# Gate halves over both attentions, an output granule between the channel means, and the third norm's token factor behind the products

## Chip, cores, metric

One NeuronCore of a Trainium2 chip runs the whole program. Its engines are TensorE (PE, with its weight loads as PEld), VectorE (DVE), ScalarE (ACT), GpSimd (POOL) and SyncE (SP, which only starts transfers). The metric is the device time of one execution in microseconds.

## What is computed

Two transformer blocks on 256 tokens of width 1024, everything in float32, cut here to what the change touches:

```python
# first block
h = rmsnorm(x, norm_mix)                       # first norm
y_a = dilated_mixture(qa, ka, va)              # attention "A", 8 heads
y_b = indexed_sparse_attention(qb, kb, vb, qi, ki, wi)   # attention "B", 64 best keys of each query
merged = sigmoid(h @ w_ga) * (y_a @ w_up_a) + sigmoid(h @ w_gb) * (y_b @ w_up_b)
x = x + merged @ w_out
h = rmsnorm(x, norm_ffn)                       # second norm
x = x + (silu(h @ w_gate) * (h @ w_up)) @ w_down
x = rmsnorm(x, norm_final)
# second block
h = rmsnorm(x, norm1_g)                        # third norm
q, k, v, a, gate = split(h @ w_in)             # q and k are normed by head and rotated
attn = attention(q, k, v)                      # attention "G", 8 query heads, 2 key heads
c = silu(layernorm(conv31(a * sigmoid(gate)))) # 512 channels, 31 taps
x = x + concat([attn, c]) @ w_out
hn = rmsnorm(x, norm2_g)
x = x + experts(hn)       # 8 heads choose 16 of 16384 rows of u and of v each
x = rmsnorm(x, final_g)
```

## The kernel before

**Precision.** A float32 product is made of three products of parts: each weight granule (128 x 2048, 1 MB, in the order of the list `GRANULES`) is loaded by SP into one of three `raw` buffers, ACT copies it to `w_hi` (`prepare`), POOL subtracts to get `w_lo` (`low_part` of POOL, four pieces), and PE multiplies high by high, high by low and low by high. The activations are split likewise, by ACT or DVE (`high_of_...`) and DVE (`low_of_...`). Only the query weights of the experts are used whole.

**Order.** Each engine runs its own program in order; semaphores tie them together. PSUM has eight banks. `plan_psum` writes down the order in which PE fills which bank, and `ps.start`, `ps.full`, `ps.empty` and `ps.copied` wait and signal by that plan; the orders of the engines are written out by hand. DVE and ACT queue whatever stands behind a wait.

**Attentions.** `attention(kind, ...)` exists on PE, DVE and ACT and goes through eight units (two tiles of 128 tokens, four pairs of heads). In step s PE makes the scores, transposes the probabilities of unit s - 1, and multiplies them by the values at steps 3, 5, 8 and 9; the factors of the softmax are turned at steps 6 and 9. DVE takes the maxima, ACT the exponentials. In A, DVE also picks the best keys for B (`select_round`). Beside this PE computes the gates (`gate_half`, two halves of 24 products to a granule) and the first part of the up products (`up_products`, 12 products each); `gate_beside` says which half goes with which step: in A one in every step 0 to 8, in B in steps 0 to 6, then `up_products` in steps 7 and 8 and behind. In G, PE also does 28 of the taps of the fourth group of channels, DVE most of the others, POOL 16 taps of the third group; `mean_of_conv` and `var_of_conv` form the layer norm's sums on PE, and DVE subtracts the mean and multiplies.

**Third norm.** `both_sums` on ACT forms the sums of squares of x and of x times `norm_final` (called `hn`); the product of the final norm of the first block and of the third norm is one factor for each token. DVE scales `hn` by it (`down_norm`, `scaled_tokens`), PE turns the scaled tokens (`turn_piece(2, ...)`, with small products of `keep_warm` in the meantime), DVE multiplies by the gain of each channel, and the parts feed the products `kv2`, `conv0` to `conv3` and `q2`. DVE's `conv_input` writes a times the sigmoid; `head_roots` (ACT) and `head_norm` (DVE) norm the heads.

**Behind G.** `out2` is the output product of the second block, granules `wp0` to `wp3`, each by tile of tokens (`high_tokens`, `out_products`). Then come the queries and the experts: DVE chooses, POOL gathers 128 rows of 4 KB with each instruction, DVE forms the dot products with u, PE adds the rows of v.

## Time and profile before

| | us |
|---|---|
| median of three runs | 1261.77 (1257.54 to 1262.18) |
| the profiled execution, its time | 1261.23 |
| the profiled execution, its span | 1259.3 |

| engine | busy us | share of the span |
|---|---|---|
| PE | 1036.7 | 82% |
| PEld | 673.7 | 53% |
| DVE | 772.0 | 61% |
| ACT | 412.1 | 33% |
| POOL | 885.1 | 70% |

The profile is one execution. Engines work side by side, so the shares don't add up. A line of a timeline gives the start in us from the span's beginning, the length, the engine, the line of the kernel, the operation with output and inputs, how many instructions were merged (x8), and in brackets the idle time of the engine before it with what ended it. Ends of matmuls are modelled. The granted clock is the share of TensorE's full 2.4 GHz that was granted (0.50 is 1.2 GHz throughout). Rough stages: first projections to 82 us, A to 120, B to 157, up and output products to 205, feed-forward to 390, third norm and second projections to 437, G to 474, output and queries to 595, experts to the end; the first gather starts at 493.58.

### The profile page before, as it was taken

The numbers are of one execution on the slowest core, as the hardware profiler recorded it, in microseconds if no ns is written. First come the engines' busy times: TensorE is split into PE (matmuls) and PEld (weight loads), VectorE is DVE, ScalarE is ACT, GpSimd is POOL, SyncE is SP. The second block draws the span as 40 slices with busy tenths as digits, with TensorE's granted clock in tenths as the row PEclk, the third lists the DMA queues.
The fourth block names the chain that finished last, engine by engine and source line by source line (L and its number), as shares of the span: only waits on it lengthen the run. The fifth ranks groups of instructions, "written<-read, shape, count | busy, mean of one in ns | idle before, by whom it ended". The sixth has DMA issues, their size and how long they took to land.

```text
span 1259.3 us, 13029 instructions
## 1 busy us (share of the span) xinstructions
PE 1036.7 (82%) x4236; PEld 673.7 (53%) x4236; DVE 772.0 (61%) x1708; ACT 412.1 (33%) x764; POOL 885.1 (70%) x827
## 2 busy tenths in 40 slices
PE   7999899999999989768887868568595785856875
PEld 7889788888888967757332323223141331322322
DVE  4466344566797786558875845547484663655445
ACT  5466655443437563113031121202121021221231
POOL 6866487999996893554757667676676766757664
PEclk9999999999999999878988879688796987979889
DMA  7634255554554427887999999899999989989997
GB/s 272 200 135 147 89 168 188 181 199 172 196 205 164 163 105 263 292 329 262 352 339 406 341 348 399 331 410 332 381 369 347 401 336 360 391 333 409 345 360 312
DMA packets 89727, 356.80 MB, mean 283 GB/s; under 512 B 9680, under 2 KB 9808, under 8 KB 82384
## 3 DMA queue, kind: packets, MB, share of 16 engines
q0 software_dynamic: 73728, 268.47, 55.6%
q1 hardware_dynamic: 15520, 86.15, 19.5%
q10 hardware_dynamic: 432, 1.57, 0.3%
q8 instruction: 27, 0.44, 0.1%
q14 instruction: 20, 0.16, 0.0%
HBM read 355.10 MB, written 1.05 MB: 283 GB/s over the span
## 4 chain that ended last, share of the span: by engine, by line
PE 34%; POOL 25%; issue 21%; DVE 8%; another core or an unknown queue 6%; DMA 4%; ACT 1%; POOLq 0%; SPq 0%; DVEq 0%; ACTq 0%
PE bank L1359 9%; POOL u_row L2727 9%; POOL v_row L2727 8%; POOL w_lo L2678 8%; PE bank L903 7%; PE bank L905 3%; DVE u_row L2510 3%; PE bank L738 3%; PE bank L739 3%; PE bank L740 3%; PE bank L825 2%; DMA u_row<-peer_u_dram,expert 1%; DMA v_row<-peer_v_dram,expert_of_v 1%; PE bank L1278 1%
## 5 line engine op out<-in xcount | busy, mean ns | idle before, releaser
L1359 PE MATMUL bank<-v_row,diag 128*128 128x512 f32 x928 | 463.5, 645 | 168.1 <-issue 147.3
L1359 PEld LDWEIGHTS bank<-v_row,diag 128*128 128x128 f32 x928 | 187.7, 205 | 443.5 <-issue 418.7
L2678 POOL TENSOR_TENSOR w_lo<-raw,w_hi 128x512 fp32r<-128x512 f32 (+1 forms) x280 | 367.2, 1352 | 80.1 <-ACT w_hi L1498 80.0
L2510 DVE CUSTOM_DVE_ANT_0 u_row<-u_row,bank 128x1024 f32<-128x1024 f32 x256 | 301.7, 1213 | 89.5 <-DMA u_row<-peer_u_dram,expert 55.4
L2727 POOL DMA_INDIRECT v_row<-peer_v_dram,expert_of_v x240 | 231.2, 963 | 157.2 <-remote 81.0
L2727 POOL DMA_INDIRECT u_row<-peer_u_dram,expert x256 | 244.6, 956 | 116.0 <-issue 73.4
L1793 ACT ACTIVATE diag<-consts,mixw 128x128 f32<-128x128 f32 x256 | 79.4, 389 | 504.5 <-remote 352.3
L1498 ACT ACTIVATE w_hi<-raw 128x2048 fp32r<-128x2048 f32 x71 | 135.8, 1912 | 74.0 <-PE bank L740 29.1
L903 PE MATMUL bank<-hT_high_and_low,w_hi 128*128 128x512 f32 x352 | 124.6, 399 | 0.0
L905 PE MATMUL bank<-hT_high_and_low,w_lo 128*128 128x256 f32 x352 | 98.8, 281 | 0.0
L903 PEld LDWEIGHTS bank<-hT_high_and_low,w_hi 128*128 128x128 f32 x352 | 66.1, 188 | 16.6 <-POOL w_lo L2678 0.6
L905 PEld LDWEIGHTS bank<-hT_high_and_low,w_lo 128*128 128x128 f32 x352 | 66.5, 189 | 0.0
L738 PE MATMUL bank<-hT_high_and_low,w_hi 128*128 128x256 f32 x192 | 55.8, 290 | 0.0
L740 PE MATMUL bank<-hT_high_and_low,w_lo 128*128 128x256 f32 x192 | 54.3, 283 | 0.0
L739 PE MATMUL bank<-hT_high_and_low,w_hi 128*128 128x256 f32 x192 | 54.3, 283 | 0.0
L825 PE MATMUL bank<-w_hi,hT_high_and_low 128*128 128x512 f32 (+1 forms) x224 | 50.2, 376 | 0.0
L1288 PE MATMUL bank<-hT_whole,raw_late 128*128 128x256 f32 x160 | 39.6, 397 | 11.0 <-issue 11.0
L825 PEld LDWEIGHTS bank<-w_hi,hT_high_and_low 128*128 128x128 f32 x224 | 39.5, 188 | 8.0 <-issue 0.7
L1288 PEld LDWEIGHTS bank<-hT_whole,raw_late 128*128 128x128 f32 x160 | 31.5, 199 | 17.6 <-issue 13.8
L2201 DVE TENSOR_REDUCE ff_up<-bank 128x256 f32<-128x512 f32 x22 | 15.2, 690 | 38.9 <-PE bank L905 38.9
L738 PEld LDWEIGHTS bank<-hT_high_and_low,w_hi 128*128 128x128 f32 x192 | 36.6, 190 | 2.0 <-issue 1.5
L739 PEld LDWEIGHTS bank<-hT_high_and_low,w_hi 128*128 128x128 f32 x192 | 36.6, 191 | 0.0
(300 smaller groups left out, 1468.5 us busy)
## 6 DMA issues: line engine op xcount, KB each, us to landing
raw<-stream_dram SPq DMA_DIRECT2D x74, 1024.0 KB, 4.8
u_row<-peer_u_dram,expert POOLq DMA_INDIRECT x256
v_row<-peer_v_dram,expert_of_v POOLq DMA_INDIRECT x240
raw_late<-stream_dram SPq DMA_DIRECT2D x3, 1024.0 KB, 4.9
raw_late<-stream_dram SPq DMA_DIRECT2D x4, 512.0 KB, 6.1
residual<-x_in_dram SPq DMA_DIRECT2D x2, 512.0 KB, 4.0
out_dram<-residual SPq DMA_DIRECT2D x4, 256.0 KB, 2.2
consts<-consts_in_dram SPq DMA_DIRECT2D x1, 840.0 KB, 10.6
```

Of the source, the lines that this page charges most:

```text
L738: mm(out_ap, left[0], right[0], start=first, stop=False, skip_group_check=resumed)
L739: mm(out_ap, left[0], right[1], start=False, stop=False, skip_group_check=resumed)
L740: return mm(out_ap, left[1], right[0], start=False, stop=last, skip_group_check=resumed)
L825: mm(out, x[:, k, t * P:(t + 1) * P], w, start=first and k == chunks[0] and x is source[0], stop=False)
L903: mm(bank[:, :].rearrange("p (s t) -> p s t", s=2), high, hT_both[:, :, k, :], start=k == 0, stop=False, skip_group_check=True)
L905: ins = mm(bank[:, 0:T], low, hT_hi[:, k, :], start=False, stop=k == KD - 1, skip_group_check=True)
L1359: ins = mm(accs[half][:, :], diag[:, 2 * m + i, :], row[:, half * 512:(half + 1) * 512], start=False, stop=True, skip_group_check=True)
L1498: activation(w_hi[parts_slot(n)][:, :], raw[n % RING][:, :], ACT.Copy).then_inc(high_done, 1)
L1793: ins = activation(diag[:, i, :], ident, ACT.Copy, scale=mixw[:, i:i + 1])
L2510: ins = v.tensor_tensor_reduce(out=row_of_u, in0=row_of_u, in1=hn_tile[:, :], scale=1.0, scalar=0.0, op0=ALU.mult, op1=ALU.add, accum_out= ...
L2678: ins = nc.gpsimd.tensor_tensor(w_lo[r][:, cols], source[:, cols], w_hi[r][:, cols].bitcast(F32), ALU.subtract)
L2727: nc.gpsimd.indirect_dma_start(rows[2 * m + i][:, :], None, table_in, bass.IndirectOffsetOnAxis(ap=named[:, b, 2 * m + i:2 * m + i + 1], a ...
```

## The change

It has three parts. (1) Of the 16 gate halves, A takes seven (steps 0 to 4, 6 and 8) instead of nine, B nine instead of seven; `up_products(0, 0)` moves to B's step 9, the next two behind the loop, and ACT's `prepare("up1")` from step 7 to the end of step 8. (2) PE turns the unscaled `hn`, its first two turns among the last products of `w_down`; `high_of_norm(2)` on ACT moves ahead of the sums of the last piece, `prepare("conv1")` behind all sums. The token factors are formed later: DVE writes two diagonal blocks, one product spreads them to all rows (`factor_rows`), DVE copies them to `factors`; `conv_scale` multiplies both halves of each conv bank by them, v and the heads' norm take the factor as a scalar, ACT's squares as `scale`. (3) `out2` of tile 0 starts its first granule (high parts of the tokens, both parts of `wp0`) between the two halves of the channel means in G's step 7; `high_of_y("G", 0, 0)` goes ahead of that step's exponentials. Nothing is left out of the computation.

```diff
@@ -223,15 +223,12 @@
...
 PAIRED = "ABG"
-GATE_FROM = {"A": 0, "B": 9}
-UP_BESIDE = {7: 0, 8: 1, 9: 2}
+GATE_STEPS = [("A", s) for s in (0, 1, 2, 3, 4, 6, 8)] + [("B", s) for s in range(9)]
...
-    if kind == "G" or s > 8 or GATE_FROM[kind] + s >= NGATE:
-        return None
-    return divmod(GATE_FROM[kind] + s, 2)
+    return divmod(GATE_STEPS.index((kind, s)), 2) if (kind, s) in GATE_STEPS else None
...
@@ -296,8 +293,8 @@
...
                 ps.plan("D", ("gate", gate_beside(kind, s)[0]))
-            if kind == "B" and s in (7, 8):
-                ps.plan("D", ("up", UP_BESIDE[s]))
+            if (kind, s) == ("B", 9):
+                ps.plan("D", ("up", 0))
             if (kind, s) == ("A", 0):
...
@@ -782,11 +782,13 @@
...
                     ps.copied(pe, ("out", t, half))
+                elif i == 2:
+                    pe.wait_ge(gained, 2 * t + half + 1)
                 else:
-                    pe.wait_ge(normed, TT * i + 2 * t + half + 1)
+                    pe.wait_ge(normed, 2 * t + half + 1)
                 name = ("norm", i, t, half)
                 bank = ps.start(pe, name)
-                tokens_in = X if i == 1 else xs
+                tokens_in = (xs, X, hn)[i]
                 for c in range(4):
...
@@ -980,8 +982,8 @@
...
                         scores_ahead()
-                    if kind == "B" and s in (7, 8):
-                        up_products(UP_BESIDE[s], 0)
+                    if (kind, s) == ("B", 9):
+                        up_products(0, 0)
                     if kind == "G" and s == 8:
...
@@ -1002,8 +1004,12 @@
...
                         mean_of_conv(0)
+                        ps.start(pe, ("out2", 0, 0))
+                        pe.wait_ge(y_high, 2 * 2 + 1)
+                        high_tokens(0, 0)
                 if kind == "B":
-                    up_products(2, 0)
+                    for c in (1, 2):
+                        up_products(c, 0)
...
@@ -1164,6 +1190,7 @@
...
             for half in range(2):
+                turn_piece(2, 0, half)
                 done = down_part(last - 1, 1, half)
...
@@ -1187,9 +1214,6 @@
...
-            for half in range(2):
-                turn_piece(2, 0, half)
-            keep_warm(BRIDGE[2][1])
             low_part("kv")
...
@@ -1203,8 +1227,11 @@
...
             ps.fill(kv_low(1, 1), ("kv2", 1))
+            pe.wait_ge(factors_known, 2)
+            mm(y_bank[:, 0:T], mean_w, xs[:, 1, 0:T], start=True, stop=True).then_inc(factor_rows, 1)
             for c in range(2):
                 pair(f"conv{c}", ("conv", c))
+            pe.wait_ge(factors_copied, 1)
             tokens("q2", ("q20", "q21"), hT)
...
@@ -1308,10 +1315,10 @@
...
             ps.copied(pe, ("y", "G", 0))
-            for q in range(2):
-                ps.start(pe, ("out2", 0, q))
-                high_tokens(q, 0)
-                out_products(q, 0, "low tokens")
+            out_products(0, 0, "low tokens")
+            ps.start(pe, ("out2", 0, 1))
+            high_tokens(1, 0)
+            out_products(1, 0, "low tokens")
             pe.wait_ge(conv_high, 1)
...
@@ -1465,6 +1472,8 @@
...
                         prepare("conv0", 0)
+                    if (t, half) == (1, 1):
+                        high_of_norm(2)
                     ps.copied(act, ("down", t, half))
...
@@ -1503,8 +1512,6 @@
...
                         continue
-                    if i == 2 and (t, half) == (1, 0):
-                        prepare("conv1", 0)
                     act.wait_ge(ht_full, 4 * i + piece + 1)
...
@@ -1528,6 +1535,8 @@
...
                 for s in range(len(todo) + 1):
+                    if (kind, s) == ("G", 7):
+                        high_of_y(kind, base, 0)
                     if s < len(todo):
...
@@ -1542,7 +1551,7 @@
...
                         high_of_y("A", 0, 1)
-                    if s == 7:
+                    if s == 7 and kind != "G":
                         high_of_y(kind, base, 0)
...
@@ -1567,7 +1576,7 @@
...
                         prepare(f"wp{s}", 0)
-                    if kind == "B" and s == 7:
+                    if kind == "B" and s == 8:
                         prepare("up1", 0)
...
@@ -1671,13 +1680,14 @@
...
             both_sums()
-            high_of_norm(2)
+            prepare("conv1", 0)
...
                     prepare(f"conv{c}", ahead)
-                bank = ps.full(act, ("conv", c))
+                bank = ps.bank(("conv", c))
+                act.wait_ge(conv_scaled, c + 1)
                 activation(conv_b[:, c, :], bank[:, T:2 * T], ACT.Sigmoid).then_inc(conv_sig, 1)
...
@@ -1687,9 +1697,10 @@
...
                     act.wait_ge(head_sum_done, n - 1)
-                activation(relu[:, n % 2, 0:cols], bank[:, 0:cols], ACT.Square).then_inc(head_sq_done, 1)
                 if n == 0:
                     act.wait_ge(final_rstd, 1)
+                activation(relu[:, n % 2, 0:cols], bank[:, 0:cols], ACT.Square, scale=column(rstd, TT * 3 + t)).then_inc(head_sq_done, 1)
+                if n == 0:
                     activation(X[:, 0, :], hn[:, 0, :], ACT.Copy, scale=column(rstd, TT * 2)).then_inc(x_scaled, 1)
...
@@ -2249,27 +2260,25 @@
...
-            def down_norm(t):
-                norm_scale(TT * 3 + t, TT * 2 + 2 * t + 1)
-                scaled_tokens(t, hn, TT * 3 + t)
             down_tile(0)
-            down_norm(0)
-            down_tile(1)
             for half in range(2):
...
                               ps.bank(("norm", 2, 0, half))[:, :].rearrange("p (c t) -> p c t", c=4)).then_inc(ht_high, 1)
-            down_norm(1)
-            low_of_norm(2, 0, 0)
-            gain_of_norm(2, 0, 1)
-            low_of_norm(2, 1, 0)
-            gain_of_norm(2, 1, 1)
+            for half in range(2):
+                low_of_norm(2, half, 0)
+            down_tile(1)
+            for half in range(2):
+                gain_of_norm(2, half, 1)
             for half in range(2):
                 low_of_norm(2, half, 1)
+            for t in range(TT):
+                norm_scale(TT * 3 + t, TT * 2 + 2 * t + 1)
+            for t in range(TT):
+                ins = v.tensor_scalar(xs[:, 1, t * P:(t + 1) * P], ident, column(rstd, TT * 3 + t), float(CC * P), ALU.mult, ALU.mult)
+            ins.then_inc(factors_known, 1)
             dve.wait_ge(root_done, TT * 4)
...
@@ -2281,6 +2290,7 @@
...
                 settle(v.reciprocal(head_rstd[:, b, 0:heads], head_root[:, b, 0:heads]))
+                settle(v.tensor_scalar(head_rstd[:, b, 0:heads], head_rstd[:, b, 0:heads], column(rstd, TT * 3 + n % TT), None, ALU.mult))
                 whole = bank[:, 0:heads * HD].rearrange("p (h w) -> p h w", w=HD)
...
@@ -2304,9 +2314,15 @@
...
             settle(v.memset(conv_in[:, :, PAD + T:], 0.0))
+            def conv_scale(c):
+                bank = ps.full(dve, ("conv", c))
+                both = bank[:, :].rearrange("p (s t) -> p s t", s=2)
+                v.tensor_tensor(both, both, row(factors, 2, T), ALU.mult).then_inc(conv_scaled, 1)
...
-                bank = ps.full(dve, ("conv", c))
+                bank = ps.bank(("conv", c))
                 dve.wait_ge(conv_sig, c + 1)
...
@@ -2315,7 +2331,7 @@
...
                 dve.wait_ge(head_sq_done, t + 1)
-                v.tensor_copy(v2[:, t, :], bank[:, 2 * HD:4 * HD])
+                v.tensor_scalar(v2[:, t, :], bank[:, 2 * HD:4 * HD], column(rstd, TT * 3 + t), None, ALU.mult)
                 head_norm(t, bank, 2)
...
@@ -2324,6 +2340,11 @@
...
                 rotated_from(("kv2", t))
+            dve.wait_ge(factor_rows, 2)
+            settle(v.tensor_copy(factors[:, :], y_bank[:, 0:T]))
+            v.memset(flag[:, :], 0.0).then_inc(factors_copied, 1)
+            for c in range(2):
+                conv_scale(c)
             conv_input(0)
...
@@ -2335,8 +2356,10 @@
...
             for c in range(2, CC):
+                conv_scale(c)
+                conv_taps(2)
                 conv_input(c)
-                conv_taps(4)
+                conv_taps(2)
             attention("G", 2, None)
...
```

The hunks left out are the plan of the PSUM banks (`out2` of tile 0 moves from banks 0 and 2 to 2 and 0, the names behind it accordingly), two semaphores, and `out_products` and `high_tokens`, which move unchanged to where step 7 of G can call them.

## Rows read from the trace of the kernel before

**Rows 1.** Windows view, two stretches: length, busy us (instructions), granted clock, DMA share, GB/s
```profile
163.00:384.00 221.00, 220.35 (x1206) 190.07 (x1205) 145.97 (x179) 99.49 (x93) 202.64 (x151) 1.00 0.53 187
...
493.50:1259.30 765.80, 561.05 (x1364) 262.06 (x1362) 459.69 (x1152) 151.19 (x383) 491.99 (x512) 0.85 0.92 352
```

**Rows 2.** Timeline: start, length, engine, line, operation, out, in; POOL's first gather
```profile
493.58 1.15 POOL L2727 DMA_INDIRECT u_row<-peer_u_dram,expert  x1 [17.33 <-PE bank L1233]
```

**Rows 3.** Timeline of PE, ACT and DVE in the first attention, steps 5 and 6
```profile
101.10 0.36 PE L738 MATMUL bank<-hT_high_and_low,w_hi 128*128 128x256 f32 x1
...
104.06 0.60 PE L913 MATMUL bank<-consts,E_sb 128*128 128x128 f32 x4
...
102.39 0.36 ACT L1565 ACTIVATE PT<-bank 128x256 f32<-128x256 f32 x1
...
106.39 0.69 DVE L2076 SCALAR_TENSOR_TENSOR S_sb<-bank,consts 128x512 f32<-128x512 f32 x1 [1.14 <-issue]
...
109.24 0.41 DVE L2017 MATCH_REPLACE8 score<-little,score 128x256 f32<-128x256 f32 x1
```

**Rows 4.** Timeline of ACT, POOL and PE at the end of the second attention
```profile
152.12 1.90 ACT L1498 ACTIVATE w_hi<-raw 128x2048 fp32r<-128x2048 f32 x1
...
154.40 0.60 ACT L1592 ACTIVATE full<-bank 128x512 f32<-128x512 f32 x1
...
154.10 9.91 POOL L2678 TENSOR_TENSOR w_lo<-raw,w_hi 128x512 fp32r<-128x512 f32 x8 [15.13 <-ACT w_hi L1498]
...
153.53 0.66 PE L913 MATMUL bank<-consts,rden_wide 128*128 128x128 f32 x4
...
159.10 0.39 PE L738 MATMUL bank<-yT_hi,w_hi 128*128 128x256 f32 x1 [3.36 <-POOL w_lo L2678]
```

**Rows 5.** Waits of PE, 119 to 164 us: us in total, times, longest
```profile
PE bank L913 <- ACT E_sb L1539: 0.7, 1, 0.7
...
PE bank L1040 <- DVE yT_lo L2142: 0.5, 1, 0.5
```

**Rows 6.** Windows view of the five microseconds after PE's wait
```profile
160.00:165.00 5.00, 5.00 (x33) 5.00 (x33) 1.18 (x3) 2.30 (x2) 4.01 (x4) 0.72 0.68 210
```

**Rows 7.** Timeline of the third norm: roots on ACT, kv products on PE
```profile
394.18 0.48 ACT L1434 ACTIVATE root<-sumsq,var 128x1 f32<-128x1 f32 x2
...
394.28 0.71 PE L1181 MATMUL bank<-w_hi,hT_high_and_low 128*128 128x256 f32 x4 [0.26 <-DVE hT_high_and_low L2264]
...
401.47 0.64 PE L1187 MATMUL bank<-w_hi,hT_high_and_low 128*128 128x256 f32 x4
```

**Rows 8.** Timeline of DVE and POOL between the convolution's products
```profile
398.36 0.68 DVE L1910 TENSOR_TENSOR bank<-bank,params 128x512 f32<-128x512 f32 x1
...
415.07 7.53 DVE L656 SCALAR_TENSOR_TENSOR bank<-conv_in,params,bank 128x256 f32<-128x256 f32 x19
...
437.44 0.43 DVE L2311 TENSOR_TENSOR conv_in<-bank,conv_b 128x256 f32<-128x256 f32 x1 [4.06 <-ACT conv_b L1681]
...
432.17 0.94 POOL L2710 TENSOR_SCALAR conv_p<-conv_in,params 128x256 f32<-128x256 f32 x1
```

**Rows 9.** Timeline of PE, DVE, ACT and POOL at the third attention's end; one window
```profile
466.33 1.79 PE L1062 MATMUL bank<-conv_a,consts 128*128 128x256 f32 x4 [1.66 <-DVE conv_a L2124]
...
468.00:470.00 2.00, 2.00 (x11) 1.29 (x11) 1.81 (x4) 1.93 (x3) 2.00 (x3) 0.50 0.87 369
...
464.42 1.43 DVE L2122 TENSOR_TENSOR conv_a<-conv_a,conv_p 128x256 f32<-128x256 f32 x1
...
468.88 1.23 ACT L1602 ACTIVATE conv_b<-conv_a 128x512 f32<-128x512 f32 x2
...
476.83 0.64 ACT L1735 ACTIVATE yT_hi<-conv_b 128x512 fp32r<-128x512 f32 x1
...
460.62 15.63 POOL L2678 TENSOR_TENSOR w_lo<-raw,w_hi 128x512 fp32r<-128x512 f32 x12
...
479.47 1.07 PE L1233 MATMUL bank<-w_hi,yT_hi 128*128 128x512 f32 x4
```

## What I predict, and from what

> **What bounds the kernel now.** I read the table of stretches first, then for each stretch that the change touches what ended PE's idle time, then the timelines of all engines there. From 163 to 384 us PE is busy 220.35 of 221 us, from 493.5 to the end the 16 DMA engines are busy 0.92 of the time at 352 GB/s [rows 1]. So the span has two regimes. Up to the first gather PE sets the pace, with short stretches in which VectorE (DVE) or a chain through ScalarE (ACT) and GpSimd (POOL) does; every microsecond at 163 us arrives at 384, since PE stands for 0.65 us in between. After the first gather, at 493.58 [rows 2], the memory traffic is the clock, and its volume is untouched: I let a shift of the first gather pass one for one. The sum is therefore the shift of three places: PE's product of `up2` at 159.10, the start of the third attention at about 439.5, and the first gather. All numbers are of the profiled execution: span 1259.3, time 1261.23; the median of the three runs is 0.54 more, and I add the shift to that median, 1261.77.
>
> **Part 1, gate halves.** The two halves at steps 5 and 7 of the first attention leave it; the second gets them, in its steps 7 and 8, and `up0` and `up1` move behind. PE's work is the same. A half is 24 products, from 101.10 to the transpose at 104.06, 3.0 us [rows 3]; two are 6.0. What covers their place? At step 5 PE would reach the values of units 0 and 1 at 101.8, but ACT copies the fourth unit's probabilities until 102.75 [rows 3]: 1.0 idle. At step 7 the transpose waits for a bank's copy, 0.5. DVE takes 3.26 us a unit for the scores and two rounds of selection (106.39 to 109.65) [rows 3], and moves up only 1.1 us, since it was already busy; its next unit starts at about 110.0 and frees the bank that the second scores of B need at 110.7: 1.1 idle. Bank and copy waits at the end add 0.4. So of 6.0 us 3.0 come back as idle time, and PE enters the second attention 3.0 us earlier. The bounds are 0 and 6.0 us.
>
> In the second attention the added halves only cover what is idle there, but `up1` is split later. Before, ACT wrote its high part at 152.12, ahead of the copy of the last factor (154.40), POOL began at 154.10 and PE got it at 159.10 after 3.36 us of waiting [rows 4]. Now the high part stands behind the copy of that factor, and this copy waits for PE's transpose of the factor, which comes behind two gate halves and `up0`. It began at 153.53 [rows 4]; now 3.0 us earlier from A, 6.0 later for the two halves, 1.5 earlier because `up1` (12 products) goes behind it, and 1.2 earlier because the waits of 0.7 and 0.5 us [rows 5] are covered: 153.8, ending at 154.4. Queued behind the waiting copy on ACT are the high parts of `up1` and `up2`; for the first POOL waits, and PE for POOL. Copy 0.6, high part 1.98 to POOL's start, split 4.96 (half of the 9.91 us of eight pieces) [rows 4]: 162.0. PE has values and `up1`'s first half, 2.5 us, to put beside 7.6, and then waits 5.1 us. That is 2.9 us later than 159.10. With no gain in A it would be 5.9, with all of it -0.1. The granted clock, at its full 2.4 GHz before, was on average 0.72 in the 5 us after this wait [rows 6], so the products ran partly at 1.2 GHz; the longer wait brings the same fall, and it cancels. **Part 1: +2.9 us**, passed on to 384.
>
> **Part 2, the third norm.** Removed: the wait of the transposes for root, reciprocal and scaling, and the small products that keep PE busy meanwhile; the scalings themselves give way to two small ones. Two transposes of 0.45 us go between the last products of `w_down`, which end 1.0 us later. From there: kv of tile 0 at 391.3 instead of 394.28 [rows 7], transposes of tile 1 at 393.2, and the last kv product ends at 397.9 instead of 401.95 [rows 7]: 4.0 us gained. Then the change adds a wait: the factors come from the roots, which ended at 394.66 [rows 7] and now, with two copies of 0.6 us and a wait for the transposes ahead of the second half's squares, at 398.3; with a reciprocal and two scalings of 0.24 us 398.9. PE stands 1.0 us, behind it the whole of `conv0`, which then starts at 399.2, 2.7 early. `conv1` is split by 405.3 and its high part no longer precedes the roots; with 48 products of 0.12 us each and 0.3 us of waiting for that split, it ends at 411.0.
>
> DVE then takes this away. The two new `conv_scale(0)`, `conv_scale(1)` stand ahead of `conv_input(0)`, so DVE waits for `conv1` (411.05), with the first 8 taps queued behind, which had run beside `conv1`'s products. A scaling of 128x512 in PSUM has no row; the nearest is the gain multiply, 0.68 us [rows 8], bounded by the 0.43 of half the size below and by the 1.43 of the slow DVE add above [rows 8, 9]; I take 0.7. From 411.05: 0.7, input 0.4, 8 taps 4.2, input 0.4, 20 taps 8.0 (7.53 us for 19) [rows 8] = 424.9 against 422.6. Two query tiles at 4.35 + 0.2 for the added small product give 434.0, two scalings, two inputs and 8 taps 5.7: 439.8, against 439.5 (the input at 437.44 and four taps). The 4.06 us that DVE had waited for `conv3` [rows 8] are eaten up; PE, with `conv3` done at 434.5, waits for the turned queries. The rest of the additions (factor on v, ACT's `scale`, one product of 0.28 us) lies on the same instructions or beside others. ACT's copy of the keys now stands behind the sigmoid of `conv2` and ends at 435.7, still ahead. **Part 2: +0.3 us**, bounds -4.0 (the PE gain passes) and +3.8.
>
> The side effect is POOL's. It starts its 16 taps when `conv_input(2)` has freed the bank: 436.0 instead of 432.17 [rows 8], so it ends them at 464.5 instead of 460.62, and DVE's add of its part began at 464.42 [rows 9]. The wait costs 0.1 at most; behind it POOL splits `wp1` to `wp3`, done at 480.1 instead of 476.25 [rows 9]. There is no slack left at the join.
>
> **Part 3, the granule.** Eight products (1.8 us) go between the two means, where PE waited 1.66 us for DVE [rows 9]. y's high part is ready at 463.5 (it precedes the exponentials now, 0.5 us of ACT that no one misses), the granule ends at 466.9, 0.4 after the second mean could start. The granted clock was 0.50 in 468 to 470, and the second mean's four products took 1.79 us [rows 9]; with the gap filled I take them at 1.1. The variances wait for ACT's squares, from 468.88 on [rows 9], at the earliest 469.5 and 470.1: the second ends at 471.2 instead of 472.4. The rest follows: values, low tokens, `wp1` until 476.3, conv's high part at 476.4 instead of 477.4 (ACT), so `wp2` starts at 476.45 instead of 479.47 [rows 9]; 3.0 early. `wp3`'s low part is there at 480.1, needed at 480.1. With the 0.4 and the nearness of POOL I take **-2.5 us**, bounds -3.3 and +0.4.
>
> DVE's add of two SBUF operands of 128x256 took 1.43 us beside POOL, a multiply of that size with one operand in PSUM 0.43 [rows 8, 9]. The Trainium skill ("SBUF — State Buffer", section "SBUF: two separate sides") calls the shared port pair of DVE and GpSimd an exclusive lock: the loser waits for the whole instruction. It speaks against this change, because the later splits now lie beside `low_of_conv(0)`, which is on the path. By the row's excess, 1.0 us, part 3 would be -1.5; without it -2.5.
>
> **Sum:** +2.9 + 0.3 - 2.5 = +0.7 us: 1262.5.
>
> **Rivals.**
> - The norm's gain passes: if DVE's 4.06 us of waiting and POOL's chain hold more than I count, part 2 is -4.0: 1261.77 + 2.9 - 4.0 - 2.5 = 1258.2. For it: DVE is the only thing between; against it: the taps are counted instruction by instruction.
> - Everything passes: selection does not hold PE in A and `up1` meets PE, part 1 -0.1: 1255.2. Against it: the copy of the factor stands ahead of `up1` in ACT's program.
> - The join (ends slower): POOL meets DVE at 464.5 without slack. If four of DVE's instructions between 411 and 436 lose 0.95 us each (about the excess of the slow row [rows 9]), the second conv input comes 3.8 later, past the join, POOL's `wp3` at 484 swallows part 3: 2.9 + 0.3 + 3.8 = +7.0, 1268.8. It decides from the moment `conv_input(2)` ends after 435.9. Against it: these instructions have a PSUM operand.
> - The change does not do what it says: in A the halves had covered selection entirely, PE gains nothing, part 1 is +5.9: 1265.5; or the clock falls all the same at 466 and part 3 gives 0.
>
> **Chances.** Forecast 0.46 (its own range 1259 to 1266), norm's gain passes 0.14, everything passes 0.12, the join 0.10, the last 0.18. Faster by over 0.5% (6.3 us, about what a measurement here can tell from no change) means under 1255.5: everything passes, and a little of its neighbour, 0.14. Slower means over 1268.1: 0.11. Within: 0.75. The three runs spread over 4.6 us. The range reaches from the everything case to the join case: 1255 to 1268.5.
>
> **What would show it.** Part 1: PE's first `up2` product at about 162, the wait for POOL near 5 us, and 1 us waits on copies and scores in A. Part 2: kv done by 398 + 2.9, DVE without idle time between 411 and 440 (+2.9), first maximum of G near 442.6. Part 3: no 0.50 clock at the second mean, `wp2` three us closer to it. The first gather near 494.3. Wrong would be: `up2` before 160, DVE waiting for `conv3`, POOL's taps past DVE's join, or an expert stage that is not 766 us long.

## The result and the profile after

| | us |
|---|---|
| median before, same chip | 1260.36 (1257.54 to 1265.61) |
| median after | 1265.09 (1258.98 to 1271.49) |
| ratio after to before | 1.0034, 95% interval 1.0018 to 1.0050 |
| the profiled execution after, its span | 1260.9 |

The changed kernel is 4.3 us slower (0.0034 of 1260.36; the two medians alone differ by 4.7), less than the 0.5% that the forecast called no change. I had forecast +0.7 us, and the difference lies almost wholly in one of the three parts.

The profiled span grew by 1.6 us only (1259.3 to 1260.9), since the two executions differ where the change does nothing. The windows view of after, the two stretches of [rows 1] (length, busy us, granted clock, DMA share, GB/s):

```profile
163.00:384.00 221.00, 218.62 (x1198) 189.03 (x1199) 141.65 (x176) 99.04 (x90) 206.05 (x154) 0.99 0.54 187
499.30:1260.90 761.60, 569.91 (x1364) 265.73 (x1362) 459.98 (x1151) 150.27 (x383) 491.44 (x512) 0.83 0.92 354
```

The stage of the experts took 761.6 us instead of 765.8, at 354 GB/s instead of 352; and the first attention began at 86.63 us in after and 85.37 in before, though nothing had changed up to there. So I read every kernel by its first gather, less the start of its first attention. In before that is 493.58 - 85.37 = 408.21 us, in after 499.31 - 86.63 = 412.68: **4.47 us later**, which agrees with the medians. All shifts below are formed so ("net"), from one profiled execution each, against before.

```profile
499.31 1.16 POOL L2750 DMA_INDIRECT u_row<-peer_u_dram,expert  x1 [10.85 <-PE bank L1063]
```

**Part 1 in after.** The timeline of PE in the first attention (start, length, engine, line, operation, count, idle time before and what ended it), and in a second fence the windows behind the waits:

```profile
110.20 0.63 PE L915 MATMUL bank<-consts,E_sb 128*128 128x128 f32 x4 [0.39 <-ACT PT L1574]
110.76 0.71 PE L969 MATMUL bank<-kT,qT_qb 64*128 64x128 f32 x4
111.98 0.71 PE L969 MATMUL bank<-kT,qT_qb 64*128 64x128 f32 x4 [0.52 <-DVE S_sb L2087]
```

```profile
112.00:115.00 3.00, 3.00 (x17) 2.88 (x18) 2.83 (x9) 2.31 (x7) 0.00 (x0) 0.68 0.32 134
...
164.50:168.00 3.50, 3.44 (x17) 3.44 (x18) 0.00 (x0) 2.29 (x2) 3.50 (x4) 0.54 0.67 179
```

The waits are the forecast ones (1.1 us ahead of 104.15, then 0.39 and 0.52). New is the granted clock of 0.68 behind them: the gate half from 112.62 to 117.26 took 4.6 us instead of 3.1, and 1.5 of the 3.0 us gained were gone. At the second up granule PE waited 4.87 us for POOL (forecast 5.1).

**Part 2 in after.** DVE's query tiles, POOL beside them, and PE at the start of the third attention:

```profile
432.24 0.44 DVE L2293 TENSOR_SCALAR head_rstd<-head_rstd,rstd 128x8 f32<-128x8 f32 x1
...
437.06 1.19 DVE L2293 TENSOR_SCALAR head_rstd<-head_rstd,rstd 128x8 f32<-128x8 f32 x1
...
434.42 5.03 POOL L2701 TENSOR_TENSOR w_lo<-raw,w_hi 128x512 fp32r<-128x512 f32 x4 [1.77 <-ACT w_hi L1507]
...
443.02 0.63 PE L915 MATMUL bank<-consts,rotated 128*128 128x128 f32 x4 [0.94 <-ACT kT L1726]
443.58 1.13 PE L969 MATMUL bank<-kT,qT_qi 64*128 64x256 f32 x4
445.76 1.13 PE L969 MATMUL bank<-kT,qT_qi 64*128 64x256 f32 x4 [1.05 <-DVE conv_in L2327]
446.81 4.97 PE L1107 MATMUL bank<-conv_in,tap_diag 128*128 128x256 f32 x14
...
454.62 0.69 DVE L2081 TENSOR_REDUCE negmax<-bank 128x2 f32<-128x512 f32 x1 [2.05 <-PE bank L969]
```

Two things weren't in the forecast. A multiplication of 128x8 numbers took 0.44 and 1.19 us. And PE stood twice for about 1 us, its 14 taps then took 4.97 us (3.29 in the kernel before), and DVE waited 2.05 us for the next scores.

**Part 3 in after.** PE between the means:

```profile
472.49 1.13 PE L1088 MATMUL bank<-conv_a,consts 128*128 128x256 f32 x4 [1.61 <-DVE little L2125]
473.27 1.27 PE L1063 MATMUL bank<-w_hi,yT_hi 128*128 128x512 f32 x4
474.38 1.08 PE L1063 MATMUL bank<-w_lo,yT_hi 128*128 128x512 f32 x4
475.30 1.02 PE L1088 MATMUL bank<-conv_a,consts 128*128 128x256 f32 x4
...
485.10 1.15 PE L1063 MATMUL bank<-w_hi,yT_hi 128*128 128x512 f32 x4
```

The granule fills the gap, the second mean takes 1.02 instead of 1.79 us [rows 9], and `wp2` starts 11.72 us after DVE's addition of the conv parts (485.10 - 473.38; before 479.47 - 464.42 = 15.05): 3.3 us gained.

### The profile page after: what moved, and what is told of

Read it like the earlier page. It is cut to its first block, busy times and chain, and to the rows that moved or that the text cites. A ratio compares the mean times of both kernels' runs of the same rounds, so it can differ in the third digit from the quotient of the medians.

```text
span 1260.9 us, 12991 instructions
## 1 busy us (share of the span) xinstructions
PE 1046.8 (83%) x4214; PEld 676.9 (54%) x4214; DVE 775.2 (61%) x1716; ACT 411.4 (33%) x764; POOL 886.1 (70%) x827
## 3 DMA queue, kind: packets, MB, share of 16 engines
HBM read 355.10 MB, written 1.05 MB: 282 GB/s over the span
## 4 chain that ended last, share of the span: by engine, by line
PE 24%; issue 23%; DVE 23%; POOL 17%; another core or an unknown queue 8%; DMA 2%; ACT 1%; DVEq 0%; POOLq 0%; SPq 0%; ACTq 0%
DVE u_row L2533 11%; POOL w_lo L2701 11%; PE bank L905 6%; PE bank L1366 5%; POOL u_row L2750 4%; PE bank L907 3%; POOL v_row L2750 3%; PE bank L738 2%; PE bank L739 2%; PE bank L740 2%; DVE bank L656 1%; PE bank L1107 1%; DMA v_row<-peer_v_dram,expert_of_v 1%; PE bank L1285 1%
```

## The experiments

Shifts in us, net, against before. "Up" is PE's first wait behind the up products (166.92 in before), "G" the first maximum of the third attention (439.48), "join" DVE's addition of the conv parts (464.42), "gather" the first gather (493.58). The ratio is that of the times measured. 1' is part 1 with the early split of e4; "order", "filling" and "fold" are the edits of e6, e5 and e9, told below.

| kernel | parts | up | G | join | gather | ratio (95%) |
|---|---|---|---|---|---|---|
| after | 1, 2, 3 | +4.1 | +5.8 | +7.7 | +4.5 | 1.0034 (1.0018 to 1.0050) |
| e1_gate_only | 1 | +2.9 | +3.0 | +3.0 | +3.1 | 1.0020 (1.0003 to 1.0037) |
| e2_norm_only | 2 | 0.0 | +1.6 | +5.1 | +4.3 | 1.0032 (1.0009 to 1.0056) |
| e3_granule_only | 3 | 0.0 | +0.3 | +0.3 | -2.7 | 0.9996 (0.9977 to 1.0014) |
| e4_up_split_early | 1', 2, 3 | -3.5 | -1.8 | +1.7 | -1.7 | 0.9984 (0.9961 to 1.0008) |
| e5_norm_warm | 2, filling | 0.0 | +1.6 | +4.0 | +3.0 | 1.0015 (1.0006 to 1.0024) |
| e6_norm_order | 2, order | +0.7 | +1.8 | +5.3 | +4.3 | 1.0019 (1.0009 to 1.0030) |
| e7_gate_granule_early_split | 1', 3 | -3.6 | -3.4 | -3.4 | -5.2 | 0.9938 (0.9925 to 0.9952) |
| e8_all_mended | 1', 2, 3, order, filling | -3.5 | -2.6 | -0.2 | -1.5 | 0.9974 (0.9961 to 0.9986) |
| e9_norm_fold | 2, fold | +0.7 | +0.6 | +0.9 | -0.2 | 0.9994 (0.9962 to 1.0027) |
| e10_norm_fold_order | 2, fold, order | +0.8 | -1.0 | -0.8 | -1.6 | 0.9975 (0.9946 to 1.0004) |
| e11_all_mended_fold | 1', 2, 3, fold, order, filling at the mean | -3.6 | -4.9 | -4.7 | -6.7 | 0.9945 (0.9919 to 0.9971) |
| e12_no_norm_warm_mean | 1', 3, filling at the mean | -3.6 | -3.3 | -3.3 | -3.7 | 0.9960 (0.9930 to 0.9991) |

e5 to e8 ran on another chip, on which the experts' stage moved 403 GB/s and the kernel before took 1170.16 us; up to the first gather the timelines there have the same durations. e1 to e4 and e9 to e12 ran on two others (1264.48 and 1264.40 us before). The small shifts at "up" where part 1 isn't in (+0.7, +0.8) are the length of the slow clock behind the same wait of 3.36 us; a shift of 0.8 us is therefore the noise of this table. At the gather the three parts alone sum to 3.1 + 4.3 - 2.7 = +4.7, and the whole change gave +4.5. On the way they agree less well: at "up" after is 1.2 us later than e1, and between G and the join it loses 1.9 us where e2 loses 3.6. The clock fell in other places and for other lengths, and part of the agreement at the end is luck.

### Each part alone

e1, e2 and e3 are the kernel before with one part of the diff above each, nothing else.

> The kernel before with part 1 alone: the gate halves of steps 5 and 7 of the first attention moved to steps 7 and 8 of the second, the products of up0 and up1 behind them. Everything is taken net of the start of the first attention. My theory after reading the changed kernel's trace: the first product of the second up granule comes 4.2 us later than in the kernel before, 2.9 of it the sum of the prediction (waits of about 1.1, 0.4 and 0.5 us in the first attention, a wait of about 4.9 us for GpSimd at the end of the second), 1.3 to 1.5 because the granted clock falls behind those small waits, so that the gate half after them takes about 4.6 us instead of 3.1. The kernel ends 4 us later, ratio about 1.003. Rival, the prediction's own sum: 2.9 us, the gate half takes 3.1 and the clock stays at 1.00 between 112 and 117 us.

Measured: +2.7 us at PE's first product of the second up granule (162.64 - 86.23 against 159.10 - 85.37), +2.9 behind the up products, +3.1 at the gather. The rival, the prediction's own sum, was right; my theory, that the clock falls here too, was wrong. A window of e1 in the first attention, and PE's line at the end of the second:

```profile
112.00:115.00 3.00, 3.00 (x26) 2.88 (x25) 2.79 (x10) 2.71 (x7) 0.00 (x0) 1.00 0.18 74
```

```profile
162.64 0.58 PE L736 MATMUL bank<-yT_hi,w_hi 128*128 128x256 f32 x1 [4.88 <-POOL w_lo L2677]
```

Behind the same three small waits (0.51 us the longest here, 0.52 in after) the clock stayed at 1.00. So the 0.68 in after is not a property of the change: behind the same idle time the clock fell in one execution and not in another. The other five kernels with part 1 (e4, e7, e8, e11, e12) had it at 1.00 too.

> The kernel before with part 2 alone: the third norm's token factor applied behind the products. My theory: PE gains 3 to 4 us at the last product of kv, and VectorE's chain takes it away: the first maximum of the third attention comes 1.4 us later than before, and the first gather some 3 us later, because the granted clock falls again while the first taps of the third attention run (after two waits of about 1 us at its start). Rival, the prediction's sum: +0.3 us and no fall of the clock. A second rival: the clock fall in the changed kernel needs part 1's shift of the transfers; then +1.4 at the first gather.

Measured: +1.6 at G, +5.1 at the join, +4.3 at the gather (some 3 expected); the theory held, and the fall of the clock needs nothing of part 1. PE and DVE of e2 at the start of the third attention, and two windows there:

```profile
438.22 0.63 PE L917 MATMUL bank<-consts,rotated 128*128 128x128 f32 x4 [0.94 <-ACT kT L1722]
438.78 1.13 PE L971 MATMUL bank<-kT,qT_qi 64*128 64x256 f32 x4
440.95 2.00 PE L971 MATMUL bank<-kT,qT_qi 64*128 64x256 f32 x4 [1.04 <-DVE conv_in L2323]
442.89 5.74 PE L1085 MATMUL bank<-conv_in,tap_diag 128*128 128x256 f32 x14
448.46 0.60 PE L917 MATMUL bank<-consts,E_sb 128*128 128x128 f32 x4
...
451.46 0.69 DVE L2077 TENSOR_REDUCE negmax<-bank 128x2 f32<-128x512 f32 x1 [3.69 <-PE bank L971]
```

```profile
442.00:444.00 2.00, 2.00 (x6) 1.17 (x5) 2.00 (x6) 1.22 (x5) 1.79 (x3) 0.50 0.91 279
444.00:446.00 2.00, 2.00 (x6) 1.59 (x5) 2.00 (x6) 0.56 (x3) 1.76 (x3) 0.50 1.06 430
```

Two waits of about 1 us, then six microseconds at 1.2 GHz, in which the scores take 2.00 instead of 1.13 us and the taps 5.74 instead of 3.29. DVE, which bounds this stage, stands for 3.69 us.

From the join to the gather e2 wins 0.9 us back, although part 2 changes nothing there. POOL and DVE of e2 at the join show why:

```profile
469.22 1.27 POOL L2697 TENSOR_TENSOR w_lo<-raw,w_hi 128x512 fp32r<-128x512 f32 x1
...
470.21 0.56 DVE L2129 TENSOR_TENSOR conv_a<-conv_a,conv_p 128x256 f32<-128x256 f32 x1
```

The addition that I count as the join took 1.43 us in before [rows 9] and 0.56 here. In all 14 traces it took between 0.56 and 1.51 us and ended 0.27 to 0.29 us after the end of the splitting instruction that POOL was running. So up to 0.9 us of a shift at the gather depend on how far POOL has got with that instruction when DVE arrives.

> The kernel before with part 3 alone: the first output granule's products on the high part between the two channel means. My theory: from VectorE's add of the conv parts to the first product of wp2 3.3 us are gained, so that the first gather is 3.0 to 3.3 us earlier than before, net of the start of the first attention. Rivals: the prediction's -2.5, -1.5 if the shared port lock of the page on SBUF takes 1 us on low_of_conv, and 0 if the clock falls between the means all the same.

Measured: 0.3 at the join, -2.7 at the gather, so 3.0 us gained, the lower end of the theory and 0.5 more than the prediction. DVE's `low_of_conv(0)`, for which one rival priced POOL at 1 us, took 1.01 us instead of 0.69 in before: 0.3 us, and none in e7, which has part 3 as well (0.69).

### The late split

e4 is the changed kernel with

```diff
-                    if kind == "B" and s == 8:
+                    if kind == "B" and s == 7:
                         prepare("up1", 0)
```

> The changed kernel with one number different: ScalarE writes the high part of the second up granule at the end of step 7 of the second attention, as before the change, instead of behind the copy of the last factor in step 8. My theory: the high part is there some 4 us earlier, GpSimd's split ends before PE arrives, the wait of 4.9 us goes and with it the clock of 0.54 behind it: the first up2 product 4.5 to 5 us earlier than in the changed kernel and a first gather 5 us earlier, so the kernel is slightly faster than the one before. Rival: the split then delays the copy of the last factor and with it y, so that 2 us or more of waiting stay (gain 2 to 3 us). Second rival: the time saved comes back as idle time of PE before 384 us (gain 0).

Measured: the wait of 4.9 us is gone; PE goes through all up products from 157.57 to 165.02 without a break, at a clock of 1.00 from 160 to 164.5, and its next wait is this one:

```profile
165.70 0.36 PE L738 MATMUL bank<-yT_hi,w_hi 128*128 128x256 f32 x1 [0.69 <-DVE merged_lo L2175]
```

That is 7.6 us earlier than in after at "up" (+4.1 to -3.5): 4.9 for the wait, and the rest the slow clock behind it and in A. At the gather 6.1 us arrive, 5 had been expected; whether the kernel is faster than before, its interval (0.9961 to 1.0008) leaves open. What the forecast took for the price of moving two gate halves was the price of one number in ACT's program.

### The clock at the start of the third attention

e5 is e2 with small products whose result nobody reads:

```diff
+            warm_in(("scores",) + units("G")[0], 6)
             ps.copied(pe, ("turn", "k2"))
             turn_queries("q2", 1, 13, tiles=(1,))
             for u in range(2):
                 scores("G", 2, qT["q2"], keys_of_g, u)
+                if u == 0:
+                    warm_in(("probs",) + units("G")[0], 7)
```

> The kernel before with part 2 alone, as in e2_norm_only, and with 13 small products whose result nobody reads in PE's two waits at the start of the third attention (0.94 us for the copy of the turned keys, 1.04 us for the last conv_input). Times net of the start of the first attention, against the kernel before. In e2_norm_only the granted clock was 0.50 from 442 to 448 us, VectorE then waited 3.69 us for the scores of the third unit, and the join of the conv parts was 5.12 us late. My theory: the idle time of those two waits brings the clock down; with it filled the clock stays at 1.00, the wait of 3.69 shrinks under 0.5 us, the join is 1.6 us late and the first gather 0.8 us. Rival: the clock follows something else (the transfers of 400 GB/s that run at that time), the fall stays and the join is 5.1 us late again. Second rival: the taps wait for conv_input all the same, and VectorE's 3.69 us are part of that: join 3.5 to 4 us late at a clock of 1.00.

PE of e5 (L781 is the filling):

```profile
438.95 1.60 PE L781 MATMUL bank<-consts 128*128 128x128 f32 x12 [1.03 <-DVE conv_in L2331]
440.39 0.60 PE L917 MATMUL bank<-consts,rotated 128*128 128x128 f32 x4
440.92 1.13 PE L971 MATMUL bank<-kT,qT_qi 64*128 64x256 f32 x4
441.98 1.83 PE L781 MATMUL bank<-consts 128*128 128x128 f32 x14
443.74 1.13 PE L971 MATMUL bank<-kT,qT_qi 64*128 64x256 f32 x4
444.79 3.29 PE L1085 MATMUL bank<-conv_in,tap_diag 128*128 128x256 f32 x14
```

The clock was 1.00 in every stretch from 436 to 450 us, beside transfers of 400 GB/s, so the transfers are not what brings it down. But the join is 4.0 late, not 1.6. The second rival had that number, by another cause: I had mis-sized the filling. The first group began only when the wait was over (its bank came free at the same moment) and added 1.60 us, the second took 1.83 instead of 1.04. From the second scores to the next transpose PE needed 4.2 us (443.74 to 447.92) instead of 7.5 in e2 (440.95 to 448.46): the slow clock had cost 3.3 us, and the filling, which put the second scores 2.2 us later, took that much of it away again.

The nine kernels with part 2 agree on the clock. In the four in which PE stood for both waits (after, e2, e4, e6: 0.93 to 1.84 us and 1.04 to 1.05) it fell to 0.50 behind them; in the two with the filling, and in e9 to e11 below, whose only wait there is 0.40 to 0.57 us, it stayed at 1.00.

### The order of DVE's chain

```diff
-            for c in range(2):
-                conv_scale(c)
+            conv_scale(0)
             conv_input(0)
-            conv_taps(lead)
+            conv_taps(lead - 2)
+            conv_scale(1)
+            conv_taps(2)
             conv_input(1)
```

> The kernel before with part 2 alone, and in it VectorE's conv_input(0) and six taps ahead of conv_scale(1), instead of both scalings ahead of conv_input(0). My theory: the wait of 2.10 us for the products of conv1 in VectorE goes, since the taps of conv0 cover it, and conv_input(1) comes 1.5 to 2 us earlier than in e2_norm_only, net of the start of the first attention; PE's wait of 1.21 us ahead of q2 goes; the first maximum of the third attention is 0 to 0.5 us later than before the change instead of 1.57. PE's waits there remain, so the clock falls and the join is still 3 to 4 us late. Rival: the sigmoid's wait for the scaling, now in the open, eats the gain and nothing changes. Second rival: with VectorE earlier PE does not wait for conv_input, the clock stays up, and the join is 0 us late or earlier than before.

Half a hit. DVE's wait of 2.10 us went, and PE's of 1.21 ahead of `q2`; `conv_input(1)` came 1.1 us earlier than in e2 (1.8 less the shift of 0.7 at "up"). Yet G was as late as in e2, which only the first rival had said, for another reason. The gain vanished in the multiplication by the token factor in the head norm, which took 2.29 and 0.62 us in the two query tiles (0.44 and 1.19 in e2). POOL and DVE of e6:

```profile
424.90 6.32 POOL L2698 TENSOR_TENSOR w_lo<-raw,w_hi 128x512 fp32r<-128x512 f32 x5
...
426.46 2.29 DVE L2289 TENSOR_SCALAR head_rstd<-head_rstd,rstd 128x8 f32<-128x8 f32 x1
```

POOL's five instructions follow each other every 1.25 us and end at 426.2, 427.5, 428.7, 430.0 and 431.2. DVE's small one ends at 428.75, with one of them. The same in e2, POOL and DVE, twice:

```profile
401.44 8.82 POOL L2697 TENSOR_TENSOR w_lo<-raw,w_hi 128x512 fp32r<-128x512 f32 x7 [3.77 <-ACT w_hi L1505]
...
425.30 2.55 POOL L2697 TENSOR_TENSOR w_lo<-raw,w_hi 128x512 fp32r<-128x512 f32 x2
...
399.68 0.48 DVE L2276 TENSOR_SCALAR normed_tokens<-consts,rstd 128x128 f32<-128x128 f32 x2
...
403.08 0.95 DVE L2289 TENSOR_SCALAR head_rstd<-head_rstd,rstd 128x2 f32<-128x2 f32 x1
...
427.44 0.44 DVE L2289 TENSOR_SCALAR head_rstd<-head_rstd,rstd 128x8 f32<-128x8 f32 x1
```

POOL's pair ends at 427.85, DVE's instruction at 427.88. At 399.68 POOL is idle (3.77 us before 401.44), and the same operation on 128x128, 16 times the size of 128x8, takes 0.24 us. In the six kernels that have them (after, e2, e4, e5, e6, e8) all 24 of these small instructions end 0.02 to 0.04 us behind the end of one of POOL's. I read it so: such a `tensor_scalar` with both operands in SBUF waits until POOL is through with its running instruction (in e6 and e8 once with a second one, for which I have no reason); beside it the reciprocals of the same column took 0.17 to 0.20 and those with an operand in PSUM their usual 0.7 us. The Trainium skill ("SBUF — State Buffer", section "SBUF: two separate sides", under "Who interferes with whom") says that `tensor_scalar` between two places in SBUF can enter a mode that takes the port pair shared with GpSimd, as an exclusive lock held for a whole instruction. These rows agree with it. I had cited this lock in the prediction, but only for `low_of_conv(0)` in part 3, where it cost 0.3 us at the most. At the small instructions of part 2 I had not looked for it.

### The fold

e9 is e2 with that factor multiplied in along with the heads' own, in PSUM; e10 has the order of e6 as well.

```diff
-                settle(v.tensor_scalar(head_rstd[:, b, 0:heads], head_rstd[:, b, 0:heads], column(rstd, TT * 3 + n % TT), None, ALU.mult))
                 whole = bank[:, 0:heads * HD].rearrange("p (h w) -> p h w", w=HD)
-                settle(v.tensor_tensor(whole, whole, each(head_rstd[:, b, 0:heads], heads, HD), ALU.mult))
+                settle(v.scalar_tensor_tensor(whole, whole, column(rstd, TT * 3 + n % TT), each(head_rstd[:, b, 0:heads], heads, HD), ALU.mult, ALU.mult))
```

> The kernel before with part 2 alone, and the token factor of the head norms folded into the multiplication with the heads' factors in PSUM, instead of a small instruction of VectorE of its own (128x2 and 128x8). In e2_norm_only those four small instructions took 0.95, 1.03, 0.44 and 1.19 us, in e6_norm_order one took 2.29; each ended within 0.1 us of the end of one of GpSimd's split instructions. Times net of the start of the first attention, against the kernel before. My theory: a small instruction whose operands all lie in SBUF waits for GpSimd's running instruction, and the fold takes that wait out: the two query tiles are done 1.6 us earlier than in e2_norm_only, the first maximum of the third attention is 0 us late instead of 1.57, PE's two waits of 0.94 and 1.04 us shrink to under 0.5 each, the clock stays at 1.00 there and the join is 0 to 1 us late instead of 5.12. Rival: the waits shrink, the clock falls all the same, and the join is over 3 us late. Second rival: the folded instruction takes as much longer as the small one had cost, and nothing changes.

DVE and PE of e9, then one window:

```profile
429.41 0.76 DVE L2290 SCALAR_TENSOR_TENSOR bank<-bank,rstd,head_rstd 128x512 f32<-128x512 f32 x1
...
441.35 1.13 PE L971 MATMUL bank<-kT,qT_qi 64*128 64x256 f32 x4 [0.57 <-DVE conv_in L2322]
442.40 3.29 PE L1085 MATMUL bank<-conv_in,tap_diag 128*128 128x256 f32 x14
...
448.53 0.69 DVE L2077 TENSOR_REDUCE negmax<-bank 128x2 f32<-128x512 f32 x1 [0.37 <-PE bank L971]
```

```profile
442.00:444.00 2.00, 2.00 (x10) 1.50 (x9) 2.00 (x6) 1.62 (x6) 1.82 (x3) 1.00 1.00 399
```

The folded instruction costs 0.06 us more than the unfolded one (0.76 against 0.70). PE's first wait is gone, the second 0.57; the clock stays at 1.00, DVE's 3.69 us are 0.37, and the join is 0.9 late instead of 5.1. The theory holds: 4.2 us at the join, by way of instructions on a handful of numbers. The two in the query tiles did it; what the two in the key tiles had cost went into DVE's wait for `conv1`, 4.04 us instead of 2.10. At the join POOL is as late as DVE now: its last tap ends at 467.25, DVE's addition starts at 467.36.

> As e9_norm_fold, with the order of e6_norm_order. My theory: now the 2 us of the two small instructions in the key tiles count as well, since the taps no longer wait for conv1: conv_input(1) at 0 us against the kernel before (e6_norm_order had 1.90), the query tiles 2.9 us earlier than in e6_norm_order. From there PE, which gained some 3 us at the last product of kv, is the bound again: first maximum of the third attention 1 to 2 us earlier than before the change, join 1 to 2 us earlier, first gather 2 us earlier. Rival: PE or ScalarE holds the third attention at the time of before, 0 us. Second rival: the clock falls in PE's waits there and the join is over 1 us late.

Measured: `conv_input(1)` at -0.1, G at -1.0, gather at -1.6; less the +0.8 that this execution had at "up", G is 1.8 earlier and the gather 2.4. DVE waits again for PE there (1.96 us for the products of `conv3`), as it had in before with 4.06 [rows 8]. So part 2 is a gain in the timeline once its additions keep out of POOL's way and DVE doesn't wait for `conv1`; the interval of the ratio (0.9946 to 1.0004) just includes no change.

### Which version is best

> Parts 1 and 3 without part 2, and ScalarE's high part of the second up granule at the end of step 7 of the second attention as in e4_up_split_early. My theory: the parts add up. At the first wait of 0.3 us behind the up products it is 3.5 us earlier than before the change, and part 3 gives 3.0 us at the first gather: 6.5 us earlier net of the start of the first attention, ratio about 0.995. Rival: earlier by 3.5 us the third attention meets another limit (GpSimd's taps or VectorE) and only 4 us arrive.

The ratio is 0.9938, the lowest of all kernels here (medians 1163.30 us and 1170.16). That is 7.3 us, more than the profiled execution shows: parts 1' and 3 gave -5.2 at the gather, not -6.5. The missing 1.3 us are the clock: PE waits 1.62 us for DVE ahead of the first mean, 1.61 in e3. The windows behind it, first e3, then e7:

```profile
467.00:469.00 2.00, 2.00 (x10) 1.55 (x9) 1.70 (x4) 1.99 (x3) 2.00 (x3) 1.00 0.27 57
```

```profile
463.00:465.00 2.00, 2.00 (x6) 1.54 (x5) 1.23 (x4) 1.99 (x3) 2.00 (x2) 0.50 0.44 102
```

The granule takes 2.2 us in e3 and 3.75 in e7 (461.66 to 465.41), behind the same wait. Whether the other executions of e7 were spared this fall, no trace shows.

> All three parts with the three mends together: the early split of e4_up_split_early, the order of e6_norm_order and the small products of e5_norm_warm. My theory: the first gather is 1.7 us earlier than before (e4_up_split_early), 3.5 more by the clock and 1 to 1.5 by the order: 6 to 6.7 us earlier net of the start of the first attention, ratio 0.995, about as good as e7_gate_granule_early_split. Rival: part 2 costs at the start of the third attention all the same (VectorE's chain), and it stays 2 us or more behind e7_gate_granule_early_split.

With part 2 in the order of e6 and the filling of e5, the gather is at -1.5. Its rival was right: 3.7 us behind e7. The small instruction took 2.28 us in the first query tile here as well, and the granule ran slowly as in e7 (a clock of 0.50 in 466 to 468 us).

> e7_gate_granule_early_split with six small products whose result nobody reads in PE's wait of 1.6 us ahead of the first channel mean. In e7_gate_granule_early_split the clock was 0.50 in 463 to 465 us and the granule's eight products took 3.75 us, in e3_granule_only, behind the same wait, 2.18 at a clock of 1.00. My theory: the fall behind this wait comes in some runs and not in others; with the wait filled it does not come, the granule takes 2.2 us, and the first gather is 6.5 us earlier than before instead of 5.2. Rival: the clock falls all the same. Second rival: the small products delay the first mean, and as much is lost as is gained.

```diff
-                    ps.start(pe, ("mean",))
+                    keep_warm(6, ps.start(pe, ("mean",)))
                     pe.wait_ge(conv_done, 1)
```

Both rivals were right. The clock fell all the same, as this window of e12 shows:

```profile
464.00:466.00 2.00, 2.00 (x8) 1.73 (x7) 1.85 (x4) 1.99 (x3) 2.00 (x3) 0.50 0.45 66
```

And the small products delay the first mean: the gather is 1.5 us later than in e7. The line of e11, which has the same edit and where the clock stayed at 1.00, shows how:

```profile
460.69 1.61 PE L779 MATMUL bank<-consts 128*128 128x128 f32 x12 [1.61 <-DVE little L2125]
462.13 1.03 PE L1088 MATMUL bank<-conv_a,consts 128*128 128x256 f32 x4
```

The filling itself stood for 1.61 us behind DVE's signal and ran where the mean could have run. It covered nothing and cost 1.4 us in e11 and, partly at the slow clock, 1.9 in e12.

> All three parts with the early split of e4_up_split_early, the order of e6_norm_order, the fold of e9_norm_fold, and six small products whose result nobody reads in PE's wait of 1.6 us ahead of the first channel mean; without the small products of e5_norm_warm. My theory: 3.5 us by the early split, 1 to 2 by part 2, 3 by the granule: the first gather 7.5 to 8.5 us earlier than before net of the start of the first attention, ratio 0.993; the granule's products take 2.2 us at a clock of 1.00. Rival: part 2 gives nothing, and it equals e12_no_norm_warm_mean. Second rival: the clock falls at the start of the third attention, and it is 2 us or more worse than that one.

All parts, mended: -4.7 at the join, -6.7 at the gather, ratio 0.9945 (1258.24 us against 1264.40). The theory wanted 7.5 to 8.5; the 1.4 us of the filling are the rest. It is the earliest at the first gather of all kernels here; in the ratio e7 is as low. Without the filling I estimate another 1.4 us (462.13 - 460.69); that was not run. Against e7, which ran on another chip, the ratios don't tell (intervals 0.9925 to 0.9952 and 0.9919 to 0.9971); their timelines do, by 1.3 us at the join.

## Where the prediction was right and where not

**Part 1: right, +2.9 forecast, +2.9 to +3.1 measured alone.** In A 2.8 us were gained (to the transpose of the last factor 30.5 us in e1, 33.3 in before), 3.0 forecast. POOL's wait was 4.9, forecast 5.1. That the clock behind it cancels held within 0.2 us. What I left out is that the clock can fall behind the small waits of A; it did in the profiled execution of after (+1.5), not in the six others with part 1.

**Part 2: wrong, +0.3 forecast, +4.3 measured alone; outside my bounds of -4.0 and +3.8 by 0.5.** PE's gain was about right (`conv0` 2.1 early, forecast 2.7), and so was the reason why it doesn't pass: DVE waited 2.10 us for `conv1` in the new scalings. (The terms as written add up to 439.55, so the sum should have said +0.1.) Two steps failed. First, the term "two query tiles at 4.35 + 0.2 for the added small product": this instruction took 0.44 and 1.19, which is 1.2 us more over both tiles and as much as the whole difference at G (1.6 against 0.3). That it matches so well is partly luck: `conv1` was done 0.9 us later than forecast, and DVE's scalings, inputs and taps took 0.9 us less. Second, "the first maximum of G" was taken as the end of the story. I wrote that ACT's copy of the keys was "still ahead"; PE stood 0.94 us for it, and 1.04 for the last `conv_input`, and the clock fell to 0.50 behind that. No term of the sum stood for it, and it cost most of the 3.6 us between G and the join. The fold of e9 took both away at once. How they share the 4.2 us can be told only roughly: e5, with the clock at 1.00, still had the late DVE. Part 2 is outside the bounds by 1.3 at the join (+5.1) and by 0.5 at the gather, since the addition at the join was short in e2.

**Part 3: right in sign and mechanism, -2.5 forecast, -3.0 measured alone.** The 0.5 that I had held back for the nearness of POOL and a late second mean wasn't needed. The lock that I weighed against it cost 0.3 us at `low_of_conv(0)` in e3, not 1.0. POOL's taps in after began 9.8 us later net (443.18 and 432.17 from the start) and ended at 471.8, before DVE's addition at 473.38, because that was late too. With part 2 alone they began 5.5 us later, forecast 3.8.

**Sum.** The measured +4.3 lies inside the range that I gave, but part 2 alone is 4.0 us off, and nothing offset that: what held was the width of the range, not the +0.7. That the median after, 1265.09, lies even between 1259 and 1266 is luck: before had a median of 1260.36 in these runs, not the 1261.77 that I started from. The rivals: the join, the one that ended slower, would have come by POOL; what came was a late join too (+7.7), but by PE's clock and DVE. The gain of the norm that passes is what e10 shows, by other means than "DVE is the only thing between". The first gather passes one for one, as assumed: the medians' +4.3 are the +4.5 of the gather.

## What to carry to other kernels

A small instruction that is added to an engine's chain is not free because it is small: look at which ports it needs and what runs beside it, and fold it into an instruction that is there already. Where an edit opens a wait of a microsecond on TensorE, price the products behind it at the lower clock as well, as a possible cost. And when a step is moved behind another, look at what the moved step feeds: the late split of one granule cost more than moving the gate halves gained.

## What was new about the hardware

- A `tensor_scalar` of 128x2 or 128x8 with both operands in SBUF took 0.44 to 2.29 us beside GpSimd's split instructions of 1.3 us, and all 24 in six traces ended 0.02 to 0.04 us behind the end of one of them; with GpSimd idle, one of 128x128 took 0.24.
- VectorE's addition of 128x256 with both inputs in SBUF took 0.56 to 1.51 us beside the same instructions, and in all 14 traces ended 0.27 to 0.29 us behind the end of the one that was running.
- Two waits of TensorE of 0.9 and 1.0 us within 4 us (437.28 to 440.95) were followed by a clock of 0.50 for 6 us in e2, and by 0.50 in all four kernels that had both. The same 1.6 us of waiting ahead of the first mean were followed by 1.00 in after, e3 and e4 and by 0.50 in e7 and e8, and the same three small waits in A by 0.68 in after and 1.00 in six others. One such fall cost about 1.5 us at a gate half or a granule, and over 3 us where 14 taps stand in front of another engine's input (e2).
- Filling a wait helped only where the filling needed nothing that came with the wait's end: twice (e5's first group, e11 and e12) its bank came free at the very same moment, and it cost 1.4 to 1.9 us.
